# An encoder kernel whose gate and up products are made as seven half-width block products instead of eight

## The reference, cut to what matters

```
h = h + 0.5 * swiglu(rms_norm(h, g), w_gate, w_up, w_down)
swiglu(x) = (silu(x @ w_gate) * (x @ w_up)) @ w_down      # 1024 -> 2816 -> 1024
```

## Time and profile before

| what | value |
| --- | --- |
| timed runs | 1941.94 us median of 3 (1941.71 to 1943.26) |
| span of the profiled execution | 1941.1 us; no other time of that execution is given |
| PE busy | 1912.9 us, 99% |
| DVE busy | 1031.1 us, 53% |
| ACT busy | 635.9 us, 33% |
| POOL busy | 287.6 us, 15% |
| chain that ended last | PE 91%, DVE 5%, ACT 2%, POOL 1% |
| mean granted clock of PE | 0.997 |

### The profile page before, as it was taken

The page is one execution under the profiler, slowest core; times in us unless marked ns, Lnnn a source line. Parts: engine busy times, 40 slices in busy tenths (PEclk is TensorE's granted clock), DMA queues, the critical chain, the costliest instruction groups (busy, mean ns, idle before and its releaser), DMA issues.

```text
span 1941.1 us, 24220 instructions
## 1 busy us (share of the span) xinstructions
PE 1912.9 (99%) x8970; PEld 1543.5 (80%) x8970; DVE 1031.1 (53%) x1506; ACT 635.9 (33%) x959; POOL 287.6 (15%) x219
## 2 busy tenths in 40 slices
PE   8999999999999999999999999999989999999998
PEld 6888888777888888887888888877658888888886
DVE  5444477674644442347545442279984644442345
ACT  5323222245332222224323222234563333222222
POOL 2000001212300000224000000163243200000225
PEclk9999999999999999999999999999999999999999
DMA  4323323232223332322322332231101323322321
GB/s 175 107 86 102 104 93 109 76 101 92 87 87 106 99 97 98 109 76 94 109 90 88 109 104 92 97 113 66 55 1 44 109 86 106 99 97 98 109 76 54
DMA packets 56730, 179.59 MB, mean 93 GB/s; under 512 B 12144, under 2 KB 12144, under 8 KB 56656
## 3 DMA queue, kind: packets, MB, share of 16 engines
q1 hardware_dynamic: 54656, 173.69, 27.5%
q0 software_dynamic: 928, 3.02, 0.5%
q10 hardware_dynamic: 1088, 2.10, 0.3%
HBM read 175.04 MB, written 3.15 MB: 92 GB/s over the span
## 4 chain that ended last, share of the span: by engine, by line
PE 91%; DVE 5%; ACT 2%; POOL 1%; issue 0%; DMA 0%; DVEq 0%; SPq 0%; POOLq 0%; ACTq 0%
PE ps L1799 58%; PE ps L1817 26%; PE ps L2249 2%; PE ps L1912 1%; PE ps L2148 1%; DVE sm L1006 1%; POOL sumsq L1279 0%; ACT prob L1539 0%; PE ps L2167 0%; DVE work L982 0%; DVE stat L980 0%; PE ps L1963 0%; PE ps L1827 0%; PE ps L2198 0%; DVE rstd L398 0%
## 5 line engine op out<-in xcount | busy, mean ns | idle before, releaser
L1799 PE MATMUL ps<-x_hi,w_hi 128*128 128x512 f32 x1728 | 681.1, 394 | 8.6 <-ACT w_hi L356 7.5
L1799 PE MATMUL ps<-x_hi,w_lo 128*128 128x512 f32 x1728 | 673.8, 390 | 0.0
L1799 PE MATMUL ps<-x_lo,w_hi 128*128 128x512 f32 x1728 | 673.5, 390 | 0.0
L364 DVE TENSOR_TENSOR w_lo<-raw,w_hi 128x1024 fp32r<-128x1024 f32 x310 | 398.4, 1301 | 407.9 <-ACT w_hi L356 403.1
L356 ACT ACTIVATE w_hi<-raw 128x1024 fp32r<-128x1024 f32 x322 | 332.3, 1050 | 337.7 <-PE ps L1817 293.6
L1799 PEld LDWEIGHTS ps<-x_hi,w_hi 128*128 128x128 f32 x1728 | 325.1, 188 | 82.0 <-ACT w_hi L356 7.5
L1799 PEld LDWEIGHTS ps<-x_lo,w_hi 128*128 128x128 f32 x1728 | 325.0, 188 | 68.5 <-issue 2.4
L1799 PEld LDWEIGHTS ps<-x_hi,w_lo 128*128 128x128 f32 x1728 | 324.8, 188 | 68.7 <-DVE w_lo L364 0.8
L1817 PE MATMUL ps<-act_hi,w_hi 128*128 (+1 forms) x720 | 280.3, 389 | 0.0
L1817 PE MATMUL ps<-act_hi,w_lo 128*128 (+1 forms) x720 | 280.1, 389 | 0.0
L1817 PE MATMUL ps<-act_lo,w_hi 128*128 (+1 forms) x720 | 280.1, 389 | 0.0
(11 more groups left out here) (361 smaller groups left out, 1323.0 us busy)
## 6 DMA issues: line engine op xcount, KB each, us to landing
raw<-in_weights SPq DMA_DIRECT2D x322, 512.0 KB, 3.3
h<-in_xT ACTq DMA_DIRECT2D x4, 512.0 KB, 6.7
out<-result SPq DMA_DIRECT2D x4, 512.0 KB, 3.0
p_raw<-in_pT POOLq DMA_DIRECT2D x2, 512.0 KB, 4.2
scratch_u<-u_sc SPq DMA_DIRECT2D x1, 512.0 KB, 6.7
u_grp<-scratch_u SPq DMA_DIRECT2D x1, 512.0 KB, 4.2
scratch_y<-y_grp SPq DMA_DIRECT2D x2, 256.0 KB, 3.1
y_ch<-scratch_y SPq DMA_DIRECT2D x1, 512.0 KB, 3.6
```

The lines of the kernel that those rows point to most:

```text
L364: dve.tensor_tensor(w_lo[:, slot], raw[:, slot], w_hi[:, slot].bitcast(F32), SUB)\
L1799: last = pe.matmul(ps[:, bank], w[:, slot, k], x[:, k], start=(k == 0 and part == 0), stop=(k == KD - 1 and part == 2))
```

## The change

Four of the 22 pairs stay as they were (`PLAIN`). The other 18 (`FAST`) treat gate and up as a 2x2 block product: two blocks of weight columns (gate, up), two of the inner dimension (512 each), two of tokens (256 each), and compute it with seven products in place of eight. A product is 4 blocks x 3 matmuls with 256 moving columns, so 84 matmuls for a pair. For this

- the activations are first normalised into `xn` (ACT multiplies by the gains, POOL by `rstd`), DVE makes four mixed sums of their quarters, and all seven operands are split into high and rest parts;
- for each pair, DVE makes the two sums of two weight blocks, POOL the sum of three and the sum of four, ACT and DVE split all seven;
- ACT copies intermediate PSUM results to `part_sum` between products that go on accumulating in the same bank, and DVE adds them;
- the split of the gated product (`act_hi`, `act_lo`) of these 18 pairs moves to the down stage;
- the four sets of semaphores of the blocks become one set counted through, and `rstd` moves behind `sumsq` in memory, since `w_sum` lies over `square`, `std` and `sumsq`.

The diff, cut to its core (a line "..." stands for lines left out):

```
+PLAIN = 4
+FAST = NF - PLAIN
+HALF = T // 2
+KH = KD // 2
...
         def ffn_up_dve(dve, f, n, first):
...
+            def weight_sums(i, b):
+                slot = slot_of(first, 2 * b)
+                own = raw_half[:, 2 * slot:2 * slot + 4]
+                for k in range(2):
+                    dve.wait_ge(raw_loaded[slot + k], turn_of(first, 2 * b + k, i) * 16 + 16)
+                dve.tensor_tensor(w_sum[:, 0:2], own[:, 0:4:3],
+                                  own[:, 2].unsqueeze(1).to_broadcast([P, 2, T]), ADD)\
+                   .then_inc(fast["w_sums"], 1)
+            def sums_lo(i, b, which):
...
+                dve.wait_ge(fast["t_hi"], counted(2, f, i, b, 2 - which if opening else 1 + which))
+                dve.tensor_tensor(wf_lo[:, at], src, wf_hi[:, at].bitcast(F32), SUB)\
+                   .then_inc(fast["t_ready"], 1)
+            def own_lo(i, b, which):
...
+                dve.wait_ge(hi_ready, i * 4 + (first + 2 * b + which + 1))
+                dve.wait_ge(fast["w_more"], counted(2, f, i, b, 2))
...
+            def gate_left(i, b):
+                dve.wait_ge(fast["product"], counted(5, f, i, b, 4))
+                dve.wait_ge(fast["copied"], counted(4, f, i, b, 1))
...
+            def product(i, b):
+                dve.wait_ge(s["up_scaled"], i * 2 + (b + 1) + NF * f)
+                dve.wait_ge(s["silu_done"], i * 2 + (b + 1) + NF * f)
...
+            def residual_sums():
...
+                dve.wait_ge(fast["x_normed"], 2 * f + 2)
...
+            def fast_tile(i, b, more=True, down=False):
+                if more:
+                    weight_sums(i, b + 1)
+                    sums_lo(i, b + 1, 0)
+                gate_left(i, b)
+                if more:
+                    own_lo(i, b + 1, 0)
+                if down:
+                    split_lo(dve, first, FFN_UP)
+                up_right(i, b)
+                if more:
+                    sums_lo(i, b + 1, 1)
+                    own_lo(i, b + 1, 1)
...
+                up_left(i, b)
+                product(i, b)
             two_tiles(0, peeled=True)
-            with dve.Fori(1, NF // 2, 1) as i:
-                two_tiles(i)
+            split_lo(dve, first, 6)
+            split_lo(dve, first, 7)
+            weight_sums(2, 0)
+            residual_sums()
+            for o in range(4):
+                residual_lo(o)
+            own_lo(2, 0, 0)
+            gate(1, 0)
+            up(1, 0)
+            sums_lo(2, 0, 1)
+            gate(1, 1)
+            low(1, 0)
+            sums_lo(2, 0, 0)
+            for o in range(4, 7):
+                residual_lo(o)
+            up(1, 1)
+            own_lo(2, 0, 1)
+            low(1, 1)
+            with dve.Fori(PLAIN // 2, NF // 2 - 1, 1) as i:
+                fast_tile(i, 0)
+                fast_tile(i, 1)
+            fast_tile(NF // 2 - 1, 0)
+            fast_tile(NF // 2 - 1, 1, more=False, down=True)
...
+        def normalised(pool, f, n):
+            pool.wait_ge(rstd_ready, n + 1)
+            for half in range(2):
+                rows = slice(KH * half, KH * half + KH)
+                pool.wait_ge(fast["x_gained"], KD * f + KH * half + KH)
+                pool.tensor_tensor(xn[:, rows], xn[:, rows],
+                                   rstd[:].unsqueeze(1).to_broadcast([P, KH, T]), MULT)\
+                    .then_inc(fast["x_normed"], 1)
+        def larger_sums(pool, f, first):
+            def sums(i, b):
...
+                pool.wait_ge(fast["w_sums"], counted(1, f, i, b, 1))
...
+                pool.tensor_tensor(w_sum[:, 2], w_sum[:, 0], own[:, 3], ADD)\
+                    .then_inc(fast["w_more"], 1)
+                pool.wait_ge(fast["w_more"], counted(2, f, i, b, 1))
+                pool.tensor_tensor(w_sum[:, 3], w_sum[:, 2], own[:, 1], ADD)\
+                    .then_inc(fast["w_more"], 1)
...
         def ffn_up_act(act, f, n, first, split=True):
...
                 if peeled:
+                    gained()
                     root(act, n)
...
+            def gained():
+                if n == 0:
+                    act.wait_ge(sum_step, KD - 1)
+                for k in range(KD):
+                    act.activation(xn[:, k], h[:, k], ACT.Copy, scale=gains[:, n, k:k + 1])\
+                       .then_inc(fast["x_gained"], 1)
...
+            def sums_hi(i, b, which):
...
+                    act.wait_ge(fast["product"], counted(5, f, i, b - 1, (3, 5)[which]))
+                if which == 0:
+                    act.wait_ge(fast["w_more"], counted(2, f, i, b, 2))
...
+            def fast_tile(i, b, more=True, down=False):
+                copy_part(i, b, 0)
+                copy_part(i, b, 1)
+                copy_part(i, b, 2)
+                if more:
+                    sums_hi(i, b + 1, 0)
+                    own_hi(i, b + 1, 0)
...
+                copy_part(i, b, 3)
+                if more:
+                    sums_hi(i, b + 1, 1)
...
+                silu_left(i, b)
+                if more:
+                    own_hi(i, b + 1, 1)
+                silu_right(i, b)
...
+            def product(bank, at, hi, lo, start, stop, done):
+                for k in range(KH):
+                    cols = slice(k * P, (k + 1) * P)
+                    for part, (w, x) in enumerate(((wf_hi, hi), (wf_hi, lo), (wf_lo, hi))):
+                        last = pe.matmul(ps[:, bank, 0:HALF], w[:, at, cols], x[:, k],
...
+            def fast_tile(i, b):
...
+                pe.wait_ge(split_ready, i * 4 + (first + 2 * b + 1))
+                pe.wait_ge(fast["x_ready"], 7 * f + 5)
+                pe.wait_ge(s["silu_done"], i * 2 + (b - 1) + NF * f)
+                product(first_bank, at["B11"], *plain(4), True, False, fast["product"])
+                pe.wait_ge(fast["t_ready"], counted(2, f, i, b, 2))
+                pe.wait_ge(s["up_scaled"], i * 2 + (b - 1) + NF * f)
+                product(right_bank, at["T1"], *mixed(0), True, False, fast["product"])
+                pe.wait_ge(fast["copied"], counted(4, f, i, b, 1))
+                product(first_bank, at["T2"], *mixed(1), False, False, fast["product"])
+                pe.wait_ge(fast["x_ready"], 7 * f + 6)
+                pe.wait_ge(s["gate_scaled"], i * 2 + (b - 1) + NF * f)
+                product(left_bank, at["B21"], *plain(5), True, True, fast["product"])
+                pe.wait_ge(fast["copied"], counted(4, f, i, b, 3))
+                product(first_bank, at["T3"], *mixed(2), False, False, fast["product"])
+                pe.wait_ge(split_ready, i * 4 + (first + 2 * b + 2))
+                product(right_bank, at["B22"], *mixed(3), False, True, chunk_used)
+                pe.wait_ge(fast["x_ready"], 7 * f + 7)
+                pe.wait_ge(fast["copied"], counted(4, f, i, b, 4))
+                product(first_bank, at["T4"], *plain(6), False, True, chunk_used)
```

More of the change, by code:

```diff
@@ L457, in low @@
                     gained_lo(dve, n, k)
[L459 to L466, removed]
+            for j in range(split, steps):
                 split_lo(dve, first, AHEAD + j)
+                if f is not None:
+                    for t in range(PLAIN + 2 * j, min(PLAIN + 2 * j + 2, NF)):
+                        act_low(t)
                 if j in early:
@@ new lines, in own_hi @@
+            def own_hi(i, b, which):
+                slot = slot_of(first, 2 * b)
+                at = halves_of(first, b)[("own", "B22")[which]]
+                src = raw_half[:, 2 * slot:2 * slot + 2] if which == 0 else raw_half[:, 2 * slot + 3]
+                act.wait_ge(raw_loaded[slot + which], turn_of(first, 2 * b + which, i) * 16 + 16)
+                if isinstance(i, int) and 2 * i + b == PLAIN:
+                    act.wait_ge(chunk_used, first + (5, 8)[which])
+                elif which == 0:
+                    act.wait_ge(fast["product"], counted(5, f, i, b - 1, 4))
+                else:
+                    act.wait_ge(chunk_used, i * 4 + (first + 2 * b - 1))
+                act.activation(wf_hi[:, at], src, ACT.Copy).then_inc(hi_ready, 1)
@@ new lines, in ffn_up_act @@
+            two_tiles(0, peeled=True)
+            split_hi(act, first, 6)
+            split_hi(act, first, 7)
+            for o in range(4):
+                residual_hi(o)
+            own_hi(2, 0, 0)
+            silu(2, 0)
+            sums_hi(2, 0, 1)
+            product_hi(2, 0)
+            silu(3, 1)
+            sums_hi(2, 0, 0)
+            for o in range(4, 7):
+                residual_hi(o)
+            own_hi(2, 0, 1)
+            product_hi(3, 1)
+            with act.Fori(PLAIN // 2, NF // 2 - 1, 1) as i:
+                fast_tile(i, 0)
+                fast_tile(i, 1)
@@ new lines, in ffn_up_act, with down_act, act_high @@
+            fast_tile(NF // 2 - 1, 0)
+            fast_tile(NF // 2 - 1, 1, more=False, down=True)
+        def down_act(act, n, first, steps, after=None, at=AFTER, split=0, early={}, then=None, f=None):
+            def act_high(t):
+                s = ffn_sems
```

(9 more changed lines are left out.)

210 lines of the change are left out of this document (171 added, 39 removed).

## The result

| kernel | median | runs | ratio to before, 95% interval |
| --- | --- | --- | --- |
| before | 1942.25 us | 4 | |
| after | 2019.23 us | 4 | 1.0396 [1.0380, 1.0411] |

The changed kernel is 4.0% slower, 77 us. The forecast was 2004, 3.2% slower; the time lies 15 us above it and inside its own range.

The account below looks back on a forecast made before the run. PE set the pace before; DVE's turn would afterwards. Blocks 0 to 3 lose 20.7, 12.9, 15.3 and 12.9, sum 61.8 on 1941.1: 2002.9; median 0.8 above span, 2004 us. Own range 1975 to 2040; 8 in 10: 1937 to 2058.

Parts of the forecast that it names:

- PE's new pair: Fast pairs: 84 matmuls of 256 columns at 120 ns take PE 10.1 us, against 10.88 before.
- The turn of DVE: Fast loop: DVE, POOL and ACT work in series, 10.9 us a pair, above PE's 10.1, so this sets the pace.
- The transition chain: Once per block, from the last peeled split to the first `fast_tile`: DVE's work and waits take 28 us.
- pair 4 starts 6 to 12 us late: Block 1, the first fast pair: sign that the forecast is right, PE starting it 6 to 12 us late.
- POOL's blocking: Peeled pairs: POOL's two 2048-column normalising instructions, 4.7 us each, delay DVE by 5 us, bounds 0 and 9.
- `std` late: Block 0: eight gained copies ahead of the root make `std` 5.1 us later; block 2: 2.4 us later.
- The tail: End of a gate and up stage: 9.3 us to `sums_lo`'s end, then six products of 8.7, 18.0 us.
- Clock: Transition stall drops PE to 1.2 GHz, pair 4 partly at half speed; covered by DVE's pace, uncovered 2 us a block.
- Rival 1: Fast loop and transition: DVE's turn falls to 10.3 us, uncontended port, transition 25.7 instead of 33; 1934 us; chance 0.16.
- Rival 2: Fast pairs: half-width matmuls do not hide their weight load; 2120 us at 150 ns, 2340 at 188; chance 0.06.
- rival 3: Fast loop: POOL's link is longer, 1.66 us a sum, turn 11.6, 48 us more: 2052 us; chance 0.10.
- rival 4: Transition: 9 us blocked and low clock uncovered, 24 us more: 2028 us, inside the forecast's range; no separate chance.

Follow-up runs that it names:

- `weight_sums` earlier: On the changed kernel, DVE issues the sums of the pair after the next ahead of `up_left` and `product`; 1963.02 us, 1.0105 of before.
- the kernel of the three together: Changed kernel with DVE making the large sums, POOL normalising in eight pieces and ACT's root ahead of the gains; 1941.35 us, 0.9992 of before.
- the fastest kernel, with six plain pairs: The kernel of the three together with `PLAIN` 6 instead of 4 and the residual work spread among the plain pairs; 1910.09 us, 0.9832 of before.
- the eight pieces: On the changed kernel, POOL normalises in eight instructions of 512 columns instead of two of 2048; 2004.99 us, 1.0322 of before.
- the earlier root: On the changed kernel, ACT runs `root` (making `std`) before the eight gained copies instead of after; 2011.86 us, 1.0356 of before.
- DVE's sums: On the changed kernel, DVE makes the sums of three and four weight blocks and POOL none; 1956.22 us, 1.0071 of before.
- two rests moved into waits: On the fastest kernel, with six plain pairs, `residual_lo(2)` and `residual_lo(3)` go one step earlier, into DVE waits; 1911.41 us, 0.9839 of before.

## Why the prediction was right, point by point

- **PE's new pair** was right: 120 ns a matmul, 10.08 us. The time of PE is not what decides.
- **The turn of DVE** was right: 10.9 predicted, 10.99 measured, and by the steps named: `weight_sums` to `sums_lo` 5.08 (5.10 predicted), the work behind it 5.86 to 5.96 (5.76). Taking the sums off POOL, both or one, or issuing them earlier, shortened the turn each time. 64 turns of the 0.1 missed make 6 us, the largest part of the 15 missed.
- **The transition chain** was right: 29.3 for 28 in block 1. What was missed is that POOL's own large sum also meets DVE there, L535 and L538 taking 2.3 instead of 1.2 us. The sign "pair 4 starts 6 to 12 us late" was missed: 572.60 is 13.8 us later than the 534.9 of before moved by the stage's 23.9. The path by which POOL's lock reaches PE already in its third plain pair, 1.6 us, was not in the sum. The experiments show the chain to be the second cause: 32.7 us for it alone.
- **POOL's blocking** was right in kind, and near in size with some luck: the last peeled split is 5.9 us late in block 1 for the 5 taken. The 5 was thought of as up to 9 less some 4 that DVE's gaps would take up. The trace has the split 2.2 and the product 3.7 us longer, 5.9 together, and no gap took up anything; they cost less than 4.7 each because POOL's first had only 2.4 us left when the split came, and the second 3.8 when the product came. The Trainium skill, SBUF — State Buffer, section "SBUF: two separate sides", states an exclusive lock for the whole instruction; by that rule up to 9 were possible. The traces agree: DVE's 1.23 and 0.69 become 3.45 and 4.38 beside instructions of 4.6 and 5.6 us and 1.39 and 1.07 beside short ones, and with `weight_sums` earlier the same is seen on short ones in the loop, 0.69 becoming 1.42. The 4.7 estimated for one instruction of POOL from the earlier trace rows fits the first, 4.61; the second took 5.58 since DVE's split came between.
- **`std` late** was right: 4.9 us in block 0 for 5.1.
- **The tail** was right: some 18.1 for 18.0. For block 1, 0.9 (blocking) + 1.3 (chain) + 1.5 (turns) + 0.1 (tail) make 3.8 of the 3.85 between 16.75 and 12.9; the other blocks missed by 3.1, 3.7 and 3.8. Together 14.5, with small terms all on one side.
- **Clock**: "covered" was right; turns of 10.94 during and after the low clock. "Uncovered 2 us a block" is borne out by the kernel of the three together, 1.2 to 2.5. That a wait of some 2 us brings the lower clock is not safe: it stayed at 1.00 with 2.0 and 1.5 us close together, and with 1.2 and 2.1 us it fell in three blocks and held in one.
- **Rival 1** had put its border at a turn of 10.4 with a short transition. It is real, at 10.08 and below: with both met the kernel is faster than before. **Rival 2** fell with 120 ns (its own steps give 2126 at 150 ns and some 2357 at 188, not 2120 and 2340), **rival 3** with 1.29 us a sum and 0.08 between, **rival 4** with 5.9 us blocked and the low clock covered.

What I had not seen is how near the other side was. PE's pair is 0.8 us shorter, 64 of them 51 us; the fastest kernel, with six plain pairs, is 32 us below before.

## What to carry to other kernels

Fewer operations on the busiest engine pay only if every other engine's turn stays below the new one; write that turn out as a list of what waits for what, and count an idle engine's wait in it like work. Handing work to a less busy engine helps only off that chain: here VectorE, the busier of the helpers, did GpSimd's sums in half the time, and taking them back made the kernel faster. Where a loop changes its form, count the set-up work against what the main engine has left to do, and give it more to do before the change of form when it runs dry. Single gains need not add up: the eight pieces and the earlier root, worth 14.2 and 7.4 us alone, gave 14.9 together on top of DVE's sums.

## What the runs showed of the hardware

- DVE and POOL, each with two operands in SBUF, took turns by whole instructions in every trace looked at here (DVE's split ended 1.08 us after POOL's first instruction, POOL's second 4.47 after the split). Eight pieces of 512 columns in place of two of 2048 took POOL 13.38 us for 10.16, the difference being its waits for DVE, and gave the kernel 14 us.
- The same stall of 2.1 us inside the first fast pair was followed by a granted clock of 0.59 to 0.62 in three blocks and of 1.00 in the fourth of the same execution (two rests moved into waits).
- At the lower clock (0.50, 1.2 GHz) the 256-column matmuls follow each other at 0.213 us (15 distances between 86.33 and 89.53 in the kernel with two rests moved), at the full one at 0.120; so their distance grows by a factor of 1.8 and not 2. Two of the changed kernel's:

```profile
573.40 0.41 PE L2149 MATMUL ps<-x_hi,w_hi 128*128 128x256 f32 x1
573.61 0.41 PE L2149 MATMUL ps<-x_lo,w_hi 128*128 128x256 f32 x1
```
